# Experts' rows added to the token rows by the scatter, in a two-layer hybrid decoder trunk

## The reference, cut to what matters

```python
hdn = silu(xb @ w1[e]) * (xb @ w3[e])
ys = hdn @ w2[e]                                    # each expert's rows
out = zeros.at[slot_tok].add(ys * slot_w[:, None])  # summed per token
h = h + out
```

## Time and profile before

| | us |
|---|---|
| runs of the kernel before (median; three runs) | 1525.36 (1523.56, 1525.36, 1529.0) |
| the profiled execution: its own time | 1526.16 |
| its span in the trace | 1524.3 |
| TensorE busy | 1392.2 (91%) |
| ACT busy / POOL busy / DVE busy | 506.7 / 498.7 / 429.2 |

### The profile page before, as it was taken

The page is one execution under the profiler, slowest core; times in us unless marked ns, Lnnn a source line. Parts: engine busy times, 40 slices in busy tenths (PEclk is TensorE's granted clock), DMA queues, the critical chain, the costliest instruction groups (busy, mean ns, idle before and its releaser), DMA issues.

```text
span 1524.3 us, 18860 instructions
## 1 busy us (share of the span) xinstructions
PE 1392.2 (91%) x7446; PEld 962.1 (63%) x7446; DVE 429.2 (28%) x1022; ACT 506.7 (33%) x843; POOL 498.7 (33%) x248
## 2 busy tenths in 40 slices
PE   5999999999999799878799999999999978988784
PEld 5889877788887333323388988777888863333232
DVE  3232644410214111110433335443112241111116
ACT  4522466622333111111253326664233322111111
POOL 4533433465641111110154433334655311111100
PEclk9999999999999799989899999999999979999997
DMA  6622222234363999999853222222434559999993
GB/s 237 243 84 84 70 69 70 74 100 159 103 230 141 388 418 416 416 416 417 320 196 135 83 84 76 70 69 70 158 105 157 235 202 390 416 417 417 415 417 125
DMA packets 133713, 331.20 MB, mean 217 GB/s; under 512 B 16085, under 2 KB 89861, under 8 KB 115192
## 3 DMA queue, kind: packets, MB, share of 16 engines
q1 hardware_dynamic: 123832, 310.08, 53.7%
q0 software_dynamic: 9792, 19.89, 3.4%
HBM read 312.16 MB, written 33.55 MB: 227 GB/s over the span
## 4 chain that ended last, share of the span: by engine, by line
PE 73%; SPq 11%; DMA 8%; DVE 4%; ACT 2%; issue 1%; POOL 0%; DVEq 0%; POOLq 0%; ACTq 0%
PE ps L505 18%; PE ps L506 17%; PE ps L507 17%; PE ps L842 10%; SPq L435 8%; DMA w<-in_w 3%; SPq L429 3%; DMA yb<-y_dram 2%; PE ps L671 2%; PE ps L651 1%; PE ps L659 1%; DMA y_dram<-yy,toks 1%; PE ps L607 1%; DMA xg<-x_dram,toks 1%; PE ps L834 1%
## 5 line engine op out<-in xcount | busy, mean ns | idle before, releaser
L505 PE MATMUL ps<-uH,ringH 128*128 128x512 f32 x720 | 281.9, 392 | 0.0
L506 PE MATMUL ps<-uL,ringH 128*128 128x512 f32 x720 | 280.4, 389 | 0.0
L507 PE MATMUL ps<-uH,ringL 128*128 128x512 f32 x720 | 280.3, 389 | 0.0
L842 PE MATMUL ps<-w,xT 128*64 128x512 f32 x1024 | 246.5, 637 | 36.3 <-DMA w<-in_w 33.8
L842 PEld LDWEIGHTS ps<-w,xT 128*64 128x64 f32 x1024 | 83.1, 147 | 196.1 <-issue 192.7
L1203 POOL TENSOR_TENSOR ringL<-raw,ringH 128x2048 fp32r<-128x2048 f32 (+1 forms) x32 | 142.7, 4464 | 122.6 <-ACT ringH L954 122.6
L505 PEld LDWEIGHTS ps<-uH,ringH 128*128 128x128 f32 x720 | 135.2, 188 | 28.9 <-issue 0.7
L507 PEld LDWEIGHTS ps<-uH,ringL 128*128 128x128 f32 x720 | 135.2, 188 | 28.7
L506 PEld LDWEIGHTS ps<-uL,ringH 128*128 128x128 f32 x720 | 135.2, 188 | 27.5
L842 PE MATMUL ps<-w,hT 128*64 128x512 f32 x512 | 121.4, 618 | 30.1 <-ACT hT L1148 30.1
L1250 POOL TENSOR_TENSOR ringL<-raw,ringH 128x2048 fp32r<-128x2048 f32 x32 | 147.0, 4595 | 5.1 <-ACT ringH L1082 5.1
(11 more groups left out here) (248 smaller groups left out, 2058.9 us busy)
## 6 DMA issues: line engine op xcount, KB each, us to landing
w<-in_w SPq DMA_DIRECT2D x192, 1024.0 KB
raw<-in_w_in SPq DMA_DIRECT2D x54, 1024.0 KB, 5.2
y_dram<-attT SPq DMA_DIRECT2D x8, 1024.0 KB, 11.7
braw<-in_w_branch SPq DMA_DIRECT2D x32, 256.0 KB, 4.5
raw<-in_w_out SPq DMA_DIRECT2D x8, 1024.0 KB, 5.3
yb<-y_dram SPq DMA_DIRECT2D x8, 1024.0 KB, 20.0
h_dram<-hs SPq DMA_DIRECT2D x2, 2048.0 KB, 11.2
hs<-h_dram SPq DMA_DIRECT2D x2, 2048.0 KB, 9.8
```

The source lines that it names most:

```text
L505: mm(o, h, rh, start=first, stop=False)
L506: mm(o, h, rl_, start=False, stop=False)
L507: return mm(o, l, rh, start=False, stop=last)
L842: ins = mm(o[r], lhs[:, r], rhs[x], start=first, stop=last, skip_group_check=True)
```

## The change

`y_dram`, its zeroing, its reading back and `sum_rows` are gone. The token rows are written to `h_dram` by POOL as soon as they are complete (`keep_rows`), and each scatter adds its rows to them in device memory (`compute_op=ALU.add`). Since two adding scatters may touch the same row, each waits for the one before, and the first waits for all `keep_rows`. NS is 15: pair 14 is scattered too, and only pair 15 goes through `combine`, with 2 products for each block. After scatter 14 SP loads `hs` from `h_dram`, and the closing adds wait for it tile by tile (`h_back`). The list of the choices' rows falls away: `toks` has one number for each slot, for gather and scatter alike.

```diff
-SLOTS, NS = 3, NP - 2
+SLOTS, NS = 3, NP - 1
...
-    yH = [sb(f"yH{x}", [P, D], f32r, R_O + 4 * x * KB) for x in range(2)]
+    yH = sb("yH", [P, D], f32r, R_O + 4 * (NS % 2) * KB)
...
-    yL = [sb(f"yL{x}", [P, D], f32r, R_T1 + 4 * x * KB) for x in range(2)]
-    tok_of = [sb(f"tok_of{x}", [P, S], f32r, R_T1 + (8 + 2 * x) * KB) for x in range(2)]
+    yL = sb("yL", [P, D], f32r, R_T1)
+    tok_of = sb("tok_of", [P, S], f32r, R_T1 + 8 * KB)
...
-    yb = [sb(f"yb{t}", [P, 2, D], f32, off) for t, off in
-          enumerate((R_RH + 8 * KB, R_T1 + 16 * KB, R_RH + 16 * KB, R_RH + 24 * KB))]
...
-                if u == 5:
-                    hold(sp, att_cleared.h, att_cleared.at(lay, 1))
-                    for t in range(NT):
-                        sp.dma_start(y_dram[2 * P * t:2 * P * (t + 1), :].rearrange("(p c) n -> p (c n)", c=2),
-                                     attT[:].rearrange("p h t i -> p (h t i)")).then_inc(y_zeroed.h, 16)
...
             hold(sp, down_filled.h, down_filled.at(lay, NS))
             sp.dma_start(g1[:], a["c_next_gain"][ds(lay, 1), :].partition_broadcast(P)).then_inc(g1_in.h, 16)
-            for x in range(2):
-                hold(sp, y_stored[x].h, y_stored[x].at(lay, 16 * (NS // 2)))
+            hold(sp, y_stored.h, y_stored.at(lay, 16 * NS))
             for t in range(NT):
-                if t == 2:
-                    hold(sp, up_filled.h, up_filled.at(lay, NS + 1))
-                sp.dma_start(yb[t][:], y_dram[2 * P * t:2 * P * (t + 1), :].rearrange("(p c) n -> p c n", c=2)).then_inc(y_back[t].h, 16)
+                sp.dma_start(hs[:, t, :], h_dram[t * P:(t + 1) * P, :]).then_inc(h_back[t].h, 16)
...
-                hold(pe, rows_summed.h, rows_summed.at(lay, NT))
-                combine([(tok_of[y], w[y]) for y in range(2) for w in (yH, yL)], (sum_added.h, sum_filled.h), sum_added.at(lay, -1))
+                combine([(tok_of, yH), (tok_of, yL)], (sum_added.h, sum_filled.h), sum_added.at(lay, -1))
...
-                    act.wait_ge(y_stored[p % 2].h, y_stored[p % 2].at(lay, 16 * (p // 2)))
+                    act.wait_ge(y_stored.h, y_stored.at(lay, 16 * (p - 1)))
...
+            def keep_rows(t):
+                pool.dma_start(h_dram[t * P:(t + 1) * P, :], hs[:, t, :]).then_inc(rows_stored.h, 16)
+
             for t in range(NT):
                 hold(pool, mean2_ready.h, mean2_ready.at(lay, t + 1))
                 gp_.tensor_tensor(rstd2[:, t:t + 1], ms2[:, t:t + 1], nhalf[:, 0:1], ALU.pow).then_inc(scale2_ready.h, 1)
                 hold(pool, rows_packed.h, rows_packed.at(lay, t + 1))
                 pool.dma_start(x_dram[t * P:(t + 1) * P, :], xw[:]).then_inc(u2_stored.h, 16)
+                if t < NT - 1:
+                    keep_rows(t)
...
             def scatter(p):
 
                 hold(pool, out_high.h, out_high.at(lay, p + 1))
                 hold(pool, out_low_ready.h, out_low_ready.at(lay, p + 1))
-                gp_.indirect_dma_start(y_dram, bass.IndirectOffsetOnAxis(toks[:, 1, p:p + 1], axis=0), yy[p % 2][:], None,
-                                       bounds_check=2 * S - 1, oob_is_err=False).then_inc(y_stored[p % 2].h, 16)
+                hold(pool, y_stored.h, y_stored.at(lay, 16 * p))
+                gp_.indirect_dma_start(h_dram, bass.IndirectOffsetOnAxis(toks[:, p:p + 1], axis=0), yy[p % 2][:], None,
+                                       bounds_check=S - 1, oob_is_err=False, compute_op=ALU.add).then_inc(y_stored.h, 16)
 
             hold(pool, lists_ready.h, lists_ready.at(lay, 1))
             for p in range(3):
                 gather(p)
+            keep_rows(NT - 1)
+            hold(pool, rows_stored.h, rows_stored.at(lay, 16 * NT))
             for p in range(NS):
...
-                    dve.wait_ge(y_zeroed.h, y_zeroed.at(lay, 16 * NT))
+                    dve.wait_ge(att_cleared.h, att_cleared.at(lay, 1))
...
-            def sum_rows(t):
-
-                dve.wait_ge(y_back[t].h, y_back[t].at(lay, 16))
-                link(v.tensor_tensor(hs[:, t, :], hs[:, t, :], yb[t][:, 0, :], ALU.add))
-                v.tensor_tensor(hs[:, t, :], hs[:, t, :], yb[t][:, 1, :], ALU.add).then_inc(rows_summed.h, 1)
-
             def pair(p):
                 y = p % 2
                 dve.wait_ge(silu_ready.h, silu_ready.at(lay, p + 1))
...
                     rows_copy(p + 1)
                 if p < NS:
                     if p >= 2:
-                        dve.wait_ge(y_stored[y].h, y_stored[y].at(lay, 16 * (p // 2)))
+                        dve.wait_ge(y_stored.h, y_stored.at(lay, 16 * (p - 1)))
                     dve.wait_ge(down_filled.h, down_filled.at(lay, p + 1))
                     v.tensor_copy(yy[y][:, 512:1024], bank(A[1])).then_inc(out_low_ready.h, 1)
                     return
-                if p == NP - 1:
-                    for x in range(2):
-                        last = slot_tokens(tok_of[x], slice(NS + x, NS + x + 1))
-                    last.then_inc(tokens_ready.h, 1)
-                    for t in range(1, NT):
-                        sum_rows(t)
+                slot_tokens(tok_of, slice(p, p + 1)).then_inc(tokens_ready.h, 1)
                 dve.wait_ge(out_high.h, out_high.at(lay, p + 1))
-                out_low_rows(yH[y], yL[y]).then_inc(out_low_ready.h, 1)
-                if p == NS:
-                    sum_rows(0)
...
-            dve.wait_ge(rows_summed.h, rows_summed.at(lay, NT))
             for x in range(8):
+                if x % 2 == 0:
+                    dve.wait_ge(h_back[x // 2].h, h_back[x // 2].at(lay, 16))
```

More of the change, by code:

```diff
@@ L74, in trunk @@
     x_dram = nc.dram_tensor("x_dram", (S, D), f32, kind="Internal").ap()
-    y_dram = nc.dram_tensor("y_dram", (2 * S, D), f32, kind="Internal").ap()
     R_U, R_RAW, R_RH, R_B, R_O, R_T1, R_T2, R_C = (x * KB for x in (0, 32, 64, 96, 112, 144, 176, 196))
@@ L135, in trunk @@
     hs = sb("hs", [P, NT, D], f32, R_T2)
-    rc = sb("rc", [P, 592], f32, R_T2 + 16 * KB)
+    rc = sb("rc", [P, 580], f32, R_T2 + 16 * KB)
     upper, ones, iota, slot_code = rc[:, 0:128], rc[:, 128:256], rc[:, 256:384], rc[:, 384:512]
-    group_of, second, entry = rc[:, 512:544], rc[:, 544:576], rc[:, 576:592].rearrange("p (c a) -> p c a", a=2)
+    group_of, second, tokv = rc[:, 512:544], rc[:, 544:576], rc[:, 576:580]
     wr = sb("wr", [P, KD, NR], f32, R_T2 + 18.5 * KB)
     yy = [sb(f"yy{x}", [P, D], f32, R_O + 4 * x * KB) for x in range(2)]
-    yH = [sb(f"yH{x}", [P, D], f32r, R_O + 4 * x * KB) for x in range(2)]
+    yH = sb("yH", [P, D], f32r, R_O + 4 * (NS % 2) * KB)
     xT = [sb(f"xT{x}", [P, D], f32, R_O + (8 + 4 * x) * KB) for x in range(2)]
@@ L182, in trunk @@
     den2 = small("den2", [P, 2]); rden = small("rden", [P, 2])
-    toks = small("toks", [P, 2, NP], i32); tokf = small("tokf", [P, NP])
+    toks = small("toks", [P, NP], i32); tokf = small("tokf", [P, NP])
     slot_w = small("slot_w", [P, 2, NP])
@@ L208, in trunk @@
     eid = rtmp("eid", [P, NT, 2]); pair_of = rtmp("pair_of", [P, 8, NP])
-    plan = rtmp("plan", [P, 8 * 4 * NP + 8])
+    plan = rtmp("plan", [P, 8 * 3 * NP + 8])
     def of_plan(w):
-        return (w[:, 0:256].rearrange("p (c a e) -> p c a e", a=2, e=NP), w[:, 256:512].rearrange("p (c a e) -> p c a e", a=2, e=NP),
-                w[:, 512:520])
+        return (w[:, 0:128].rearrange("p (c e) -> p c e", e=NP), w[:, 128:384].rearrange("p (c a e) -> p c a e", a=2, e=NP),
+                w[:, 384:392])
     tok_rhs, w_rhs, code = of_plan(plan)
@@ L278, in trunk @@
     u2_stored = signal("u2_stored", 16 * NT)
-    y_zeroed = signal("y_zeroed", 16 * 4); y_stored = [signal(f"y_stored{x}", 16 * (NS // 2)) for x in range(2)]
-    y_back = [signal(f"y_back{t}", 16) for t in range(NT)]; plan_kept = signal("plan_kept", 1); rows_summed = signal("rows_summed", NT)
+    rows_stored = signal("rows_stored", 16 * NT); y_stored = signal("y_stored", 16 * NS)
+    h_back = [signal(f"h_back{t}", 16) for t in range(NT)]; plan_kept = signal("plan_kept", 1)
     logits_filled = signal("logits_filled", NT)
@@ L309, in trunk @@
     block = ctx.enter_context(nc.Block())
-    DVE_LINKS, ACT_LINKS, WIN_LINKS = 195, 2, 3
+    DVE_LINKS, ACT_LINKS, WIN_LINKS = 191, 2, 3
     dve_c = signal("dve_c", DVE_LINKS)
@@ L780, in list_tile @@
                 for x in (2 * t, 2 * t + 1):
-                    last = mm(bank(A[4])[:, 256:256 + 2 * NP], slot_of[:, x, :], tok_rhs[:, x].rearrange("p a e -> p (a e)"), start=x == 0, stop=x == 7,
+                    last = mm(bank(A[4])[:, 256:256 + NP], slot_of[:, x, :], tok_rhs[:, x, :], start=x == 0, stop=x == 7,
                               skip_group_check=True)
@@ L821, in list_tokens @@
             def list_tokens(rhs):
-                return list_product(lambda x: rhs[:, x].rearrange("p a e -> p (a e)"), 256, 2 * NP)
+                return list_product(lambda x: rhs[:, x, :], 256, NP)
             def list_weights(rhs):
@@ L1162, in pair @@
                 else:
```

(16 more changed lines are left out.)

6 lines of the change are left out of this document (3 added, 3 removed).

## The result

The changed kernel took 1537.98 us (median of 5 runs, 1537.29 to 1540.43), the kernel before 1525.36 (5 runs beside it, 1523.56 to 1529.39): 1.0082 of the time before, 95% interval 1.0061 to 1.0103, 12.6 us slower. The prediction was +4.4. The profiled execution has a span of 1536.2 us against 1524.3, +11.9.

A forecast was written before the change was run, and what follows sets the result against it. The prediction took full DMA engines to bound the mixture-of-experts stage, with weights deciding. Adding scatters +17.6, layer 0's tail -5.3 and layer 1's tail -7.9 gave +4.4 us: 1530 us, range 1514 to 1548.

The forecast's parts named there:

- Full DMA engines make every MB count: In the mixture-of-experts stage, all 16 DMA engines are full, so each MB moved costs 2.40 us, whoever moves it.
- One more pass for an add, +17.6: Scatters 0 to 13 per layer: reading destination rows costs 0.63 us each, +8.8 us per layer, +17.6 in all.
- The rival of a nearly free read: Adding scatters: the destination read costs only 0 to 0.5 passes, overlapping other writes; 1513 to 1522 us; chance 0.27.
- the one of two more passes (+35): Adding scatters: a bubble between reads and write makes a row cost much more; at 2 passes 1548 us; chance 0.20.
- `keep_rows`, zeroing, the fifteenth scatter, 0: Token-row stores fit idle DMA time, dropped zeroing is worth 0, pair 14's scatter and reload stay hidden by 1 to 5 us.
- Tail of layer 1, -7.9: End of layer 1: closing products start 6.2 us sooner, and half as many products per block save 1.7 us more.
- Tail of layer 0, -5.3: End of layer 0: next layer's fills wait behind the hs loads, so ut comes at 757.4 against 762.72.
- Rival 3: Layer 0's tail gains nothing because the last scatter lands late, 12 us or more; 1534 us; chance 0.08.
- the likeliest case, 1526 to 1535: Adding scatters cost about one pass (0.8 to 1.2) with both tails as predicted: +1 to +8 us; chance 0.45.

The follow-up runs named there:

- the doubled scatters: The changed kernel with a second scatter of the same rows per pair into a spare tensor: 1563.16 us with a plain one, 1590.54 us with an adding one.
- Two fills ahead: The changed kernel with SP issuing the next layer's first two weight fills before its wait for the last scatter: 1534.17 us, 1.0057 of before.
- the kernel without POOL's adds: The kernel before with VectorE's last-pair order hid, sums 0 and 1, yL, sums 2 and 3, and no TensorE wait for rows_summed: 1521.06 us.
- the kernel with four fills ahead: The changed kernel with SP issuing all four of the next layer's first weight fills before its wait for the last scatter: 1538.14 us.

## Why the prediction was right or wrong

*Full DMA engines make every MB count: right.* (One reading there is off and carries nothing: the 0.93 in 620 to 640 is the mean granted clock, so with levels of 1.2 and 2.4 GHz the full clock was granted for 0.86 of the time.) The up product of pair 15 came 11.4 us later in layer 0, and the waits of TensorE for `w` rose from 33.8 to 51.8 us.

*One more pass for an add, +17.6: right in kind and size.* 18.0 us in the stages by the write-instead-of-add kernel; twice a plain scatter by the queue's time (41.5 us per MB plain, 83.6 adding) and by the doubled scatters. That adding also cost 2.6 us in layer 0's tail was not in this term. The rule that was weighed there, of the Trainium skill (Collectives: The Full Stack, section "Why ReduceScatter is half of AllGather"), speaks of half the bytes per time, ratio 1.93; the runs here agree with it (2.01 to 2.09). The 18.0 us do not tell one pass (+17.6) from 0.93 (+16.3). The rival of a nearly free read is excluded, and so is the one of two more passes (+35).

*`keep_rows`, zeroing, the fifteenth scatter, 0: not shown wrong, not shown exact.* The stages of the kernel that writes are 1.1 and 1.6 us longer than before. Leaving out `keep_rows` made the stage of layer 0 1.3 us shorter and that of layer 1 2.9 us longer, one trace each. It stays open whether it is a cost or spread.

*Tail of layer 1, -7.9: right, measured -8.4.* From the start of up product 15 to the closing products 15.4 us instead of 22.1 (-6.7, predicted -6.2); from there to `ut` 6.4 instead of 8.1 (-1.7 as predicted). That the gated product alone brings nothing (ratio 0.9997) shows that the gain needs the sums off the path between `hid` and the closing products. Their removal is one way; moving half of them behind `yL` gave part of it, 1.8 and 1.2 us of the tails.

*Tail of layer 0, -5.3: this step failed, measured -1.2.* The mechanism was right (weights, split, `rstd`, `ut`), the size was not. On the clock of before, shifted by the 11.4 us, the last scatter landed at 740.6 (predicted 741.6), but the first 1 MB of weights at 754.2 instead of 750.5, and `ut` came at 761.5 instead of 757.4. I had allowed 8.9 us from the scatter's landing (741.6) to the first weights (750.5), of it 0.4 until SP issues them and 8.5 until they land. It took 13.6: SP needed 3.8 us (1.8 to issue the four loads of `hs`, 2.0 in its own steps up to the fill), which the prediction had put at next to nothing, and the fill landed after 9.76, behind those loads and beside its three neighbours. With plain scatters SP needed the same 3.8 us and the fill landed after 8.45, so 1.3 of the miss comes with the adding. Rival 3 had priced nearly this (+8 in all), for another reason, a late scatter. Two fills ahead brought the tail to 22.27 us, the -7.8 that an unheld tail was worth.

The sum as measured in the traces: 18.0 for the adds, 2.7 of the stages unexplained, -1.2 and -8.4 in the tails, +0.9 elsewhere, 12.0 against 11.9 in the spans. The spans grew by 7.5 us more than the predicted +4.4: 4.1 in layer 0's tail, 3.0 in the stages (not explained but for 0.4) and 0.9 elsewhere, less 0.5 in layer 1's tail. The stated range, 1514 to 1548, was wide enough to hold this miss; the likeliest case, 1526 to 1535, was not.

## What to carry to other kernels

Where the DMA engines are full, as here (share 1.02), an add in a scatter of 4 KB rows was paid as one more pass of its rows, though the profile's bytes do not show it (24.69 MB adding, 24.60 plain); it pays only if what it removes was on the full engines or on the end's path for longer. Here 0.64 us x 28 was given for 9.6 us of tail, and without the add the tails would have gained 12.2. When a wait is put ahead of loads on a queue, count the issue time of everything between the wait and the load, and the landing among its neighbours, not only the transfer. Two of the four fills ahead of the wait helped; with all four SP was held in their issue and came late to what the wait was for. And before work is moved through memory in another form, try what its order alone gives: one `yL` between the sums and one needless wait were worth 4.2 us.

## What the runs showed of the hardware that was not expected

An adding scatter takes more of POOL than a plain one, 1.59 against 1.01 us for 128 rows, beside its double engine time.

GpSimd's and VectorE's adds of 128x1024 in float32, all operands in the SBUF, slow each other: DVE took 2.69, 3.27 and 3.27 us beside POOL against 1.22 alone, and POOL's split of the weights, begun beside the second of them, 5.56 us against 4.57 in the kernel without POOL's adds. DVE's instructions that read one operand from PSUM kept their times beside POOL: `yL` 1.22, two closing adds 1.28 us.

TensorE's granted clock fell in the middle of a fully busy stretch in some executions and not in others. Windows of the mixers of layer 1, in after and in the kernel with four fills ahead:

```profile
900.00:920.00 20.00, 20.00 (x132) 16.73 (x130) 8.54 (x12) 3.90 (x7) 7.48 (x2) 1.00 0.17 53
```

```profile
900.00:920.00 20.00, 20.00 (x106) 16.85 (x105) 9.54 (x14) 5.02 (x8) 7.48 (x2) 0.83 0.18 54
```

TensorE is busy 20.00 of 20 us in both. The mean granted clock is 1.00 and 0.83 of 2.4 GHz; with levels of 1.2 and 2.4 GHz the second stood at 1.2 for 6.8 of the 20 us. The mixers took 479.97 and 483.28 us, but 481.38 in the kernel before at 1.00 in this window, so the clock is one part of that difference only. Runs of one kernel differ by such amounts (before: 1523.56 to 1529.39), so single traces tell parts of this sum to some 3 us only. Nor was the stage equally steady: from first to last silu of layer 1 it took 221.7 to 222.1 us in five profiled kernels with plain scatters of before's form, but 233.5, 234.8, 237.5 and 237.7 in the four with the same adding scatters (after, four fills, two fills, without `keep_rows`). In layer 0 the two kinds spread alike, 220.7 to 222.9 and 230.6 to 232.1. What sets the spread of layer 1 was not tried.
